# Hybrid decoder layer on one core: gates in column groups, mask rows by DMA, another pool order, score sums in halves

## What is computed

```python
h = x @ w_in                      # columns: u (512), q, k, v, og (512 each), 4 input gates, 4 forget gates
u = h[..., :512]
ig = h[..., GATE_OFF:GATE_OFF+4] + b_i
fg = h[..., GATE_OFF+4:] + b_f
# pooling, 4 groups of 128 channels with windows 2, 4, 8, 16
diff = trailing_mean(u_g, window_g) - u_g
pool_out_g = (diff @ pool_w[g]) * pool_scale_g
# mLSTM, 4 heads of 128: a stabilised causal matrix memory
b = cumsum(log_sigmoid(fg)); a = ig - b
m = running_max(a)
s = (q @ k.T) * exp(a[s] - m[t])          # for s <= t
hm = (s @ v) / max(|s.sum|, exp(-m_t)), normalised per head
mix = concat(pool_out, sigmoid(og) * hm) @ w_out
x = layer_norm(ALPHA * x + mix)
# cross-attention, 4 heads of 256 channels, 256 memory rows; every sample has keys and values of its own
x = layer_norm(ALPHA * x + softmax(q @ mem_k.T) @ mem_v @ ca_wo)
# experts: the best of 4 groups, in it the best 2 of 4 gated MLPs
x = layer_norm(ALPHA * x + moe(x))
```

## Time and profile before

| | us |
|---|---|
| median of 3 runs | 722.62 |
| lowest, highest | 722.02, 723.19 |
| the profiled execution's own time | 720.51 |
| its span in the profile | 718.5 |
| TensorE busy | 669.3 (93%) |
| VectorE busy | 291.7 (41%) |
| ScalarE busy | 155.9 (22%) |
| GpSimd busy | 198.1 (28%) |

### The profile page before, as it was taken

One profiled execution on the slowest core, in us unless ns is written; L12 is line 12 of the kernel. 1 busy time (PEld: TensorE's weight loads), 2 busy tenths in 40 slices (PEclk: granted clock), 3 DMA queues, 4 the chain that ended last, 5 costly groups with the idle time before them and its releaser, 6 DMA issues.

```text
span 718.5 us, 8345 instructions
## 1 busy us (share of the span) xinstructions
PE 669.3 (93%) x3191; PEld 398.9 (56%) x3191; DVE 291.7 (41%) x683; ACT 155.9 (22%) x346; POOL 198.1 (28%) x230
## 2 busy tenths in 40 slices
PE   6999999999999989999999889999369999999974
PEld 4445688746788764446887764555244544333241
DVE  0370200016456883545001865256742424243346
ACT  1022312001424220002112631123303211111124
POOL 4340000000466645412001983112352222110101
PEclk9999999999999999999999999999679999999997
DMA  8983303303353253006832676553619999999366
GB/s 302 378 272 140 133 1 117 110 8 118 93 163 124 73 198 133 16 0 228 328 121 102 223 259 235 205 195 157 243 48 387 416 394 364 340 346 406 127 254 117
DMA packets 44327, 141.46 MB, mean 197 GB/s; under 512 B 5480, under 2 KB 5704, under 8 KB 40183
## 3 DMA queue, kind: packets, MB, share of 16 engines
q1 hardware_dynamic: 32663, 111.73, 42.2%
q0 software_dynamic: 9568, 24.45, 10.9%
q10 hardware_dynamic: 2056, 4.73, 1.7%
HBM read 129.68 MB, written 17.08 MB: 204 GB/s over the span
## 4 chain that ended last, share of the span: by engine, by line
PE 86%; DVE 6%; DMA 3%; ACT 2%; issue 1%; POOL 1%; ACTq 0%; DVEq 0%; POOLq 0%; SPq 0%
PE ps L390 42%; PE ps L874 12%; PE ps L423 8%; PE ps L894 6%; PE ps L940 2%; PE ps L635 2%; PE ps L690 2%; PE ps L858 1%; PE ps L706 1%; PE ps L451 1%; PE ps L526 1%; PE ps L751 1%; PE ps L620 1%; PE ps L541 1%; DVE poolw L1704 1%
## 5 line engine op out<-in xcount | busy, mean ns | idle before, releaser
L390 PE MATMUL ps<-xT,wring 128*128 128x312 f32 (+1 forms) x768 | 170.1, 383 | 0.3 <-ACT xT L1122 0.3
L390 PEld LDWEIGHTS ps<-xT,wring 128*128 128x128 f32 x768 | 139.9, 190 | 28.6 <-issue 0.8
L390 PE MATMUL ps<-wring,P 128*128 128x512 f32 x224 | 98.3, 594 | 0.0
L390 PEld LDWEIGHTS ps<-wring,P 128*128 128x128 f32 x224 | 41.9, 190 | 49.8 <-issue 49.7
L874 PE MATMUL ps<-wring,P 128*32 128x512 f32 (+1 forms) x288 | 65.2, 600 | 1.7 <-DVE P L1873 1.7
L423 PE MATMUL ps<-wring,P 128*128 128x512 f32 x128 | 55.9, 594 | 0.9 <-DVE P L1446 0.7
L1994 POOL TENSOR_SCALAR rstd<-agg 128x1 f32<-128x1 f32 (+1 forms) x15 | 16.4, 1091 | 116.3 <-DVE agg L1433 116.3
L1873 DVE COPY P<-ps 128x512 f32<-128x512 f32 x12 | 8.3, 691 | 90.5 <-PE ps L858 90.5
L874 PEld LDWEIGHTS ps<-wring,P 128*32 128x32 f32 (+1 forms) x288 | 22.2, 130 | 37.1 <-issue 37.1
L2128 POOL TENSOR_TENSOR P<-P,xT 128x2048 f32<-128x2048 f32 x8 | 36.1, 4528 | 22.7 <-DMA xT<-sq_d 18.8
L423 PEld LDWEIGHTS ps<-wring,P 128*128 128x128 f32 x128 | 24.0, 190 | 30.2 <-issue 27.5
(11 more groups left out here) (340 smaller groups left out, 973.4 us busy)
## 6 DMA issues: line engine op xcount, KB each, us to landing
wring<-in_w_in SPq DMA_DIRECT2D x5, 2048.0 KB, 9.1
wring<-in_w_gate SPq DMA_DIRECT2D x10, 1024.0 KB
wring<-in_w_up SPq DMA_DIRECT2D x10, 1024.0 KB
P<-in_w_down SPq DMA_DIRECT2D x10, 1024.0 KB, 11.2
P<-in_cache_mem_k SPq DMA_DIRECT2D x8, 1024.0 KB, 7.6
P<-in_cache_mem_v SPq DMA_DIRECT2D x8, 1024.0 KB, 4.9
wring<-in_ca_wv SPq DMA_DIRECT2D x2, 2048.0 KB, 21.7
wring<-in_w_out SPq DMA_DIRECT2D x2, 2048.0 KB, 10.3
```

Of the source, the lines that this page charges most:

```text
L390: last = mm(out, lhs(k), rhs(k), start=(k == 0), stop=(k == n - 1))
```

## The change

1. *Gates.* `wg` holds the 8 gate columns of each of the 8 channel blocks next to each other. Four channel blocks run as four groups of 32 output columns, into partitions 0, 32, 64 and 96 of one bank, in two steps. ScalarE copies the four partial sums to `parts`, and after one channel group of q a matmul with a constant matrix of zeros and ones adds them up. ScalarE makes the rows after the first q group, and the other q groups follow.
2. *Masks.* VectorE's row `mrow` is stored to DRAM and read back four times onto 128 partitions by GpSimd's queue. The mask matmuls and their waits are gone.
3. *Pools.* u is projected in the order (2, 3), (0, 1). `pool_diff` runs in the order 2, 3, 1, 0; GpSimd makes the window sum of group 0 alone, VectorE that of groups 1 to 3. The output projection takes the channel blocks 4, 5, 6, 2, 3, 1, 0, waits only for head 2's copy before it starts, and for ScalarE's pool copies before block 2.
4. *Scores.* Four of the samples' score sums are cut in halves, put behind the pairs 7, 8 and 10 to 15.

The expert stage is as it was.

```diff
+    for g in range(4):
+        for j in range(4):
+            c[32 * g + j, 340 + j] = 1.0
+            c[32 * g + 4 + j, 372 + j] = 1.0
...
+        parts = view(10964, NTOK)
+        masks_of = [smp[:, 0:512], gb[:, 0, 512:D], gb[:, 1, 512:D], view(16366, 512)]
+        sums0 = masks_of[3]
...
             for c0, cn in GRP:
                 bk = bank_a()
-                contract(bk[0:36, 0:cn], lambda k: wg[:, k, :], lambda k: xT[:, k, c0:c0 + cn]).then_inc(act_full, 1)
-            project("q", range(4))
+                for j in range(2):
+                    for g in range(4):
+                        k = 2 * g + j
+                        last = mm(bk[32 * g:32 * g + 32, 0:cn], wg[:, 8 * k:8 * k + 32], xT[:, k, c0:c0 + cn], start=(j == 0), stop=(j == 1))
+                last.then_inc(act_full, 1)
+            gate_parts = na[0]
+            project("q", range(1))
+            pe.wait_ge(act_free, gate_parts)
+            for c0, cn in GRP:
+                bk = bank_a()
+                mm(bk[0:36, 0:cn], con[:, 340:376], parts[:, c0:c0 + cn], start=True, stop=True).then_inc(act_full, 1)
+            project("q", range(1, 4))
...
             def scores(h):
-                if h >= 2:
-                    pe.wait_ge(wexp_done, NQT * (h - 1))
-                mm(MBANK[h % 2][:, :], ident[0:4, h:h + 1].broadcast_to([4, 128]), mrow[:, 0:NP_], start=True, stop=True).then_inc(mb_full, 1)
...
-            for g in range(4):
-                pe.wait_ge(dif_done, g + 1)
+            for i, g in enumerate((2, 3, 1, 0)):
+                pe.wait_ge(dif_done, i + 1)
...
             WO = ("wo0", "wo1")
-            pe.wait_ge(act_free, na[0])
-            pe.wait_ge(dve_free, nd[0])
+            pe.wait_ge(dve_free, at["heads", 2])
...
-                for k in range(KC - 1):
-                    mm(banks[-1][0:TR, :], mixT[:, k, 0:TR], w[:, k, :], start=(k == 0), stop=False)
+                for k in (4, 5, 6, 2, 3, 1, 0):
+                    if k == 2:
+                        pe.wait_ge(act_free, na[0])
+                    mm(banks[-1][0:TR, :], mixT[:, k, 0:TR], w[:, k, :], start=(k == 4), stop=False)
...
-                act.wait_ge(mb_full, h + 1)
-                mb = MBANK[h % 2]
+                act.wait_ge(mb_full, 16 * H)
+                mb = masks_of[h]
...
-            pool_diff(0)
-            carried(4)
-            carried(5)
-            pool_diff(1)
-            take_heads(2)
-            take_last(1)
-            pool_diff(2)
-            pool_diff(3)
+            pool_diff(2)
+            carried(4)
+            pool_diff(3)
+            carried(5)
+            take_heads(2)
+            take_last(0)
+            pool_diff(1)
+            pool_diff(0)
...
+            def half_scores(b, m):
+                dve.wait_ge(kq_done, b + 1)
+                last = V.tensor_reduce(sS[:, m, 4 * b:4 * b + 4], kvr[:, b % 3, m].rearrange("p (h e) -> p h e", h=4), AX, ALU.add)
+                if m == 1:
+                    last.then_inc(k_used, 1)
...
-            later = (8, 11, 13, 15)
+            later = (7, 8, 10, 11, 12, 13, 14, 15)
...
-            def window_sums(g):
+            def window_sums():
                 pool.wait_ge(act_free, at["u", 0])
-                if g == 1:
-                    pool.wait_ge(dif_done, 1)
-                add_windows(G.tensor_tensor, g, link).then_inc(usum_done, 1)
+                G.tensor_tensor(sums0, uT[:, 0, PADC:PADC + NP_], uT[:, 0, PADC - 1:PADC + NP_ - 1], ALU.add).then_inc(usum_done, 1)
...
+            pool.wait_ge(rows_dve, 2)
+            pool.dma_start(mask_d, mrow[:, 0:NP_]).then_inc(mask_out, 16)
+            pool.wait_ge(mask_out, 16)
+            for h in range(H):
+                pool.dma_start(masks_of[h], mask_d[h].partition_broadcast(128)).then_inc(mb_full, 16)
...
-            window_sums(0)
-            window_sums(1)
+            state_out(2)
             update_state(4)
             update_state(5)
+            window_sums()
             load_state(6)
-            state_out(2)
```

More of the change, by code:

```diff
@@ L75 @@
 HALF = [(0, 256), (256, 256)]
-COLS = 340
+COLS = 376
 SORT0 = COLS
@@ L585, in _ @@
             scores(2)
-            project("u", (0, 1))
-            at["u", 0] = na[0]
+            project("u", (2, 3))
+            at["u", 1] = na[0]
             transpose_heads(1)
-            transpose_last(0)
+            transpose_last(1)
             numerators(2)
@@ L592, in _ @@
             scores(3)
-            project("u", (2, 3))
-            at["u", 1] = na[0]
+            project("u", (0, 1))
+            at["u", 0] = na[0]
             transpose_heads(2)
-            transpose_last(1)
+            at["heads", 2] = nd[0]
+            transpose_last(0)
             numerators(3)
             state(3)
-            for g in range(4):
-                pe.wait_ge(dif_done, g + 1)
+            for i, g in enumerate((2, 3, 1, 0)):
+                pe.wait_ge(dif_done, i + 1)
                 for c0, cn in GRP:
@@ L1136, in _, with take_projection @@
             take_x(4)
+            for c0, cn in GRP:
+                bk = full()
+                A(parts[:, c0:c0 + cn], bk[:, 0:cn], ACT.Copy).then_inc(act_free, 1)
+            def take_projection(dstn, cts, scale, groups=GRP, off=0):
+                for ct in cts:
+                    for c0, cn in groups:
+                        bk = full()
+                        A(dstn[:, ct, off + c0:off + c0 + cn], bk[:, 0:cn], ACT.Copy, scale=scale).then_inc(act_free, 1)
+            act.wait_ge(mk_out, 64)
+            take_projection(qT, range(1), HD ** -0.5)
             act.wait_ge(small_in, 16 * 13)
-            act.wait_ge(mk_out, 64)
             for c0, cn in GRP:
@@ L1147, in _ @@
             A(trow, trow, ACT.Ln, bias=1.0).then_inc(rows_act, 1)
-            def take_projection(dstn, cts, scale, groups=GRP, off=0):
-                for ct in cts:
-                    for c0, cn in groups:
-                        bk = full()
-                        A(dstn[:, ct, off + c0:off + c0 + cn], bk[:, 0:cn], ACT.Copy, scale=scale).then_inc(act_free, 1)
-            take_projection(qT, range(4), HD ** -0.5)
+            take_projection(qT, range(1, 4), HD ** -0.5)
             act.wait_ge(rows_dve, 1)
@@ L1208, in _ @@
             finish_og((2, 3))
-            take_projection(uT, (0, 1), 1.0, off=PADC)
+            take_projection(uT, (2, 3), 1.0, off=PADC)
             take_numerators(2)
             weights(3)
-            take_projection(uT, (2, 3), 1.0, off=PADC)
+            take_projection(uT, (0, 1), 1.0, off=PADC)
             take_numerators(3)
             act.wait_ge(c_store[0], 16 * BUF.count(0))
-            for g in range(4):
+            for g in (2, 3, 1, 0):
                 for c0, cn in GRP:
@@ L1616, in _ @@
             take_heads(1)
-            take_last(0)
+            take_last(1)
             head_norm1(2)
@@ L1721, in _ @@
                 if n in later:
-                    sample_scores(later.index(n))
+                    half_scores(*divmod(later.index(n), 2))
             finish_probs(NQ - 1)
@@ L1725, in _ @@
                 take_probs(n)
-            for b in range(len(later), NS):
+            for b in range(len(later) // 2, NS):
                 sample_scores(b)
@@ L1999, in _ @@
             GO = PW + 4 * 512
-            pool.dma_start(wg[:, :, 0:4], win[:, :, GO:GO + 4]).then_inc(wgr_in, 16)
-            pool.dma_start(wg[:, :, 32:36], win[:, :, GO + 4:GO + 8]).then_inc(wgr_in, 16)
+            pool.dma_start(wg[:, 0:8 * KC].rearrange("p (k c) -> p k c", k=KC), win[:, :, GO:GO + 8]).then_inc(wgr_in, 16)
             pool.dma_start(wr[:, :, 0:4], a["w_gr"][0].rearrange("(k p) c -> p k c", p=128)).then_inc(wgr_in, 16)
@@ L2105, in _ @@
             load_state(7)
-            pool.wait_ge(dve_free, at["last u", 1])
+            pool.wait_ge(dve_free, at["last u", 0])
             pool.dma_start(o_ppool[0, 0], un[0:NPOOL, :]).then_inc(un_out, 16)
```

17 lines of the change are left out of this document (9 added, 8 removed).

## The result

The changed kernel takes 710.42 us (median of 4 runs, 709.81 to 711.51), the kernel before 722.32 us in the 4 runs beside it (721.38 to 723.19). The ratio is 0.9837, with an interval of 0.9818 to 0.9856. The profiled execution took 709.92 us, with a span of 707.8 us against 718.5.

A forecast was written before the change was run, and what follows sets the result against it. TensorE, with 86% of the chain of waits, was taken to bound the kernel. Savings of 4.4 + 2.6 + 1.9 + 1.1 = 10.0 us off 720.51, plus 2.11 to the median, gave 712.6 us (range 710.5 to 714.5, wider 708.5 to 715.5).

The forecast's parts named there:

- Gates: Gate projection: four column groups side by side take 1.8 us plus 0.9 for the sum, instead of 7.2; 4.4 saved.
- rival 3: Gate projection: the column groups run in turn, the term is 5.3 us worse, time 717.9 us; chance 5%.
- Masks: Head scores: mask matmuls go, but VectorE's banks are late next; 0.63 us in heads 1 to 3, 2.6 in all.
- the bound of 4.1: Head scores: upper bound of the mask saving in us, if VectorE is never late.
- Tail: Pools to output projection: last pool no sooner, but the output projection asks for less and starts earlier; 1.9 us saved.
- So I count the two engines one after the other: Last head stage: VectorE's 14.0 and GpSimd's 7.8 us counted in turn, so the last pool is ready at 263.5.
- Rivals 2 and 5: Last head stage: VectorE loses more to GpSimd, 715.1 us, chance 15%; or the same as a runaway, 734.1 us, 3%.
- its upper bound of 2.9: Pools to output projection: most that can be saved, in us, both TensorE waits there gone.
- Score halves: Attention loop: four score sums of 2.27 us become eight of about 1.14, taking 1.1 us off the last stall.
- the first two stalls stay: Attention loop: VectorE is loaded without a gap up to head 12, so the waits of 1.2 and 0.9 us remain.
- Rival 4: Expert stage: weights may arrive late when TensorE comes earlier, half is handed back, time 717.6 us; chance 5%.
- under about 0.2%: Whole kernel: a difference below this size (1.4 us) couldn't be told from none.

The follow-up runs named there:

- e5_relax: Kernel before with only the output projection's later wait and block order changed, pools in the old order: 720.23 us, ratio 0.9983.
- e6_order: Kernel before with only the order of u and pools changed (with its window-sum and state-store moves), old waits kept: 720.42 us, ratio 0.9967.
- e7_ring4: Changed kernel with four PSUM banks instead of three in VectorE's ring: 708.25 us, ratio 0.9785 to the kernel before.
- e10_ring4: Changed kernel with four PSUM banks in VectorE's ring, run again beside the unaltered changed kernel: 709.50 us, ratio 0.9821 to the kernel before.
- e2_masks: Kernel before with only the mask rows by DMA: 719.81 us, ratio 0.9964.
- e1_gates: Kernel before with only the gate part (column groups, split sum): 718.08 us, ratio 0.9941.
- e4_halves: Kernel before with only the score sums in halves: 722.26 us, ratio 0.9996.
- e3_pools: Kernel before with only the pools' order and the later wait of the output projection: 719.04 us, ratio 0.9948.
- e9_after: Changed kernel once more, unaltered: 710.48 us, ratio 0.9825 to the kernel before.

## Why the prediction came out

**Gates: right, 0.36 us less than forecast.** 1.96 and 1.00 us (in the chain) where 1.8 and 0.9 stood, 4.24 of saving by those two, and 4.04 in the stage; the remaining 0.2 lies at the new boundaries. Both copies lay under q, and nobody wanted the later gate rows. The column groups ran side by side; rival 3 is out.

**Masks: the mechanism right, the size 0.6 too small.** 3.2 instead of 2.6 us. The DMA rows were never late. The chain through VectorE (state bank, then one product per bank) was there, as forecast, but gave 0.73 to 0.82 a head, not 0.63, and 0.85 in head 0. With a fourth bank the wait is gone, which shows that it was the bank and not the product's own time. With four banks the gain in the heads is 5.1 us, more than the bound of 4.1. Most of the difference is a wait of the kernel before that goes as well: 0.19 us for VectorE ahead of the key transposes, in each of the four heads.

**Tail: the failed step.** "So I count the two engines one after the other" put the last pool at 263.5, as late as before. VectorE's last step (L1622) was done at 256.6 in the profile after, that is at 262.4 of the kernel before, if head 2's first copy is set equal (254.92 there, 249.16 now). From the end of head 2's normalisation the forecast had 14.0 us of VectorE, 7.8 of GpSimd, 1.1 off for the copies out of PSUM and 0.2 for hand-overs, 20.9 in all. The trace has 19.75: 5.0 lost to GpSimd (2.39, 1.13 and 1.46), 0.8 of waiting for TensorE ahead of head 2's copy, and 13.95 for the rest, which is VectorE's own work as forecast. So the term that was mis-sized is the loss to GpSimd, 6.7 where 5.0 stood in the trace. The larger part of the miss is 2.1 us of GpSimd's work (L2076 and L2077 of the second update) that fell into VectorE's waiting for TensorE and its copies out of PSUM, where the forecast allowed 1.1. The rest is that 5.7 us of it, met by VectorE's, cost only 5.0. The wait for TensorE, which the forecast didn't have, took 0.8 back.

e5_relax and e6_order split the 2.84: 1.80 by the later wait (1.9 forecast) and 1.04 by the order (0 forecast). The rule of the Trainium skill that the forecast named (SBUF — State Buffer, "SBUF: two separate sides": the two engines hold the port one at a time, for a whole instruction) agrees with this trace in the 16-column steps (2.59 and 1.63 us for 0.17), and not in the four long adds (5.26 us where the sum is 6.24). Rivals 2 and 5, which made the lock dearer still, are out. The term came close to its upper bound of 2.9, and 0.23 us more came from the output projection's first part. That goes with the later wait (14.17 in e5_relax, 14.41 in e6_order): the first 14 passes take 0.24 us longer when they start behind a hole (6.25 us in the chain of e6_order, 6.01 in that of the changed kernel). Head 3's roots weren't late: the store wait was 4.38 us.

**Score halves: the size right, the split not.** 1.27 us where 1.1 stood, with all of the 1.1 on the last stall and "the first two stalls stay". The last fell by 0.9 (1.33 to 0.43), the first by 0.5 (1.23 to 0.17 and 0.54), the second by 0.2 (0.90 to 0.72). That is 1.6 together, and TensorE's busy time in the loop came out 0.3 longer (32.79 us, 32.46 before), for which no run shows the reason. That the sum came near 1.1 is luck in part.

**Experts: right.** Nothing was handed back by weights. In the thirteen profiles of before, after and the experiments the stage took 153.3 to 157.0 us, with no tie to the edits (157.02 in e7_ring4 and 153.40 in e10_ring4, the same kernel), and the window of the earlier trace rows is unchanged. Rival 4 is out.

**The sum.** The edited stages gave 11.6 where 10.0 stood: -0.4 for the gates, +0.6 for the masks, +1.2 for the tail, +0.2 for attention. 0.9 us of that didn't show in the pair of profiles, since the first matmul, which waits for the constants, came at 5.92 instead of 4.71. Whether the 36 wider columns have a part in this is open. With the old width it came at 4.71, 5.70, 5.27, 5.21, 5.25 and 5.31 (before, e2 to e6), with the new one at 5.92, 5.75, 5.85, 5.60, 5.54 and 5.24 (after, e1, e7 to e10). The ranges overlap, the means lie 0.4 us apart. The medians of the runs are 11.9 apart, and that gap holds the spread too. The forecast's "under about 0.2%" was too fine a limit: with 10 runs against 31 the intervals are still 0.2 to 0.3% wide to each side.

## What to carry to other kernels

When two engines contend, don't choose between "in turn" and "side by side": take rows where both run at once and rows where each runs alone, and count what one loses beside the other. No single ratio carries over: long adds took 1.8 times as long (5.26 to 2.87), a 16-column step 1.63 us for 0.17. And count only the work that really meets: what falls into the other engine's waiting costs nothing. When a wait goes, follow who empties the buffer that is wanted next; a resource that the edit sets free (here a PSUM bank) is often what that next wait needs. For a microsecond in a kernel whose runs spread over ten, compare stages of the profile, and make the split (one wait alone, the order alone) in the kernel, not on paper.

## What the runs showed of the hardware

**The granted clock falls at places that vary.** In e6_order (columns as above) TensorE was busy 8.68 of 8.80 us at full clock, and then ran at 0.59 for 4.2 us, still busy all the time:

```profile
161.00:169.80 8.80, 8.68 (x97) 4.66 (x95) 3.61 (x12) 0.00 (x0) 0.00 (x0) 1.00 0.20 65
169.80:174.00 4.20, 4.20 (x12) 2.66 (x12) 2.06 (x7) 2.52 (x10) 0.59 (x2) 0.59 0.96 365
174.00:180.00 6.00, 6.00 (x30) 4.84 (x29) 5.41 (x16) 0.43 (x1) 0.57 (x2) 1.00 0.01 3
```

Between the gates and the end of the attention loop such stretches came in three places only: head 0's scores (e4_halves, e6_order), the tail (e1_gates, e2_masks), the end of the attention loop (e2_masks, e3_pools, e6_order). They cost 1.5 to 2.8 us each. Each time that place was still as in the kernel before. The kernel before and e5_relax had none, and the six profiles with the whole change had none either. Whether the change removes them or six profiles are too few, no run settles. The routing between the loop and the experts is different: TensorE waits there for a good part of the time (busy 11.51 of 22.00 us from 498 on, before), and the granted clock is low in every profile (0.77 in that window). How far this reaches into the experts explains the widest gap there: in e7_ring4 their first 6.9 us ran at 0.51 and the stage took 157.02 us, in e10_ring4, the same kernel, at 1.00 and 153.40. The spread of the run times goes with this clock: of the 11 runs of the kernel before that stand beside e9_after, the five with a mean clock of 0.978 or more had spans of 716.7 to 719.4 us, the six with 0.966 to 0.974 had 720.6 to 724.3.

**Four column groups with different moving operands run side by side.** 32 passes over 312 and 208 tokens took 1.96 us, a quarter of the 7.20 of before and 0.16 more.

**A short VectorE step can lose whole GpSimd instructions.** 16-column steps of 0.17 us took 2.59 and 1.63 beside GpSimd's work, long adds 1.8 times their time.
